# A two-block network on one core: other batch sizes for the gate projection inside the recurrent core

## The reference, cut to what matters

```python
h = rms_norm(x, norm_mix[l])
proj = h @ w_in[l]
u_pool, q, k, v, p_rw, gate_logits = jnp.split(proj, IN_SPLITS, axis=-1)
b_pool = pool_mixer(u_pool, pool_w[l], pool_scale[l])
b_da = diff_attention(q, k, v, lam, lambda_init, da_subln[l])
b_rw = rwkv7_mixer(p_rw, ...)                      # S = S*w + (S a) b + v k, token by token
branches = jnp.stack([b_pool, b_da, b_rw], axis=2)
up = jnp.einsum('blnc,ncd->blnd', branches, w_branch[l])
gates = jax.nn.sigmoid(gate_logits.reshape(B, L, 3, D_MODEL))
merged = jnp.sum(gates * up, axis=2)
x = x + merged @ w_out[l]
x = x + conv_glu_ffn(rms_norm(x, norm_ffn[l]), ...)
```

## Time and profile before

| | |
|---|---|
| median of 3 runs | 2748.31 us (2746.76 to 2751.6) |
| profiled execution: time and span | the span is 2750.0 us; the profile gives no time beside it |
| PE busy | 2680.6 us, 97% of the span |
| DVE / ACT / POOL busy | 1828.3 / 1134.2 / 354.4 us |

### The profile page before, as it was taken

One profiled execution on the slowest core, in us unless ns is written; L12 is line 12 of the kernel. 1 busy time (PEld: TensorE's weight loads), 2 busy tenths in 40 slices (PEclk: granted clock), 3 DMA queues, 4 the chain that ended last, 5 costly groups with the idle time before them and its releaser, 6 DMA issues.

```text
span 2750.0 us, 58101 instructions
## 1 busy us (share of the span) xinstructions
PE 2680.6 (97%) x25663; PEld 2454.4 (89%) x25663; DVE 1828.3 (66%) x2782; ACT 1134.2 (41%) x1844; POOL 354.4 (13%) x213
## 2 busy tenths in 40 slices
PE   8998999999999999999999999999999999999998
PEld 8987898999999999988899899999987788877886
DVE  7743345555888846844444455888845998888887
ACT  6332324534333323532424543433323346466664
POOL 1210122121111100210122121011100000010001
PEclk9999999999999999999999999999999999999999
DMA  4210222255333343211222154344332322499996
GB/s 148 81 43 23 82 77 76 71 189 183 116 128 133 127 137 124 80 54 36 59 87 82 57 173 145 100 138 134 134 101 94 93 92 69 161 359 391 390 393 257
DMA packets 113186, 372.28 MB, mean 135 GB/s; under 512 B 12560, under 2 KB 13728, under 8 KB 112544
## 3 DMA queue, kind: packets, MB, share of 16 engines
q1 hardware_dynamic: 88848, 304.04, 32.4%
q10 hardware_dynamic: 17568, 40.84, 4.2%
q0 software_dynamic: 6512, 23.62, 2.3%
HBM read 336.51 MB, written 31.94 MB: 134 GB/s over the span
## 4 chain that ended last, share of the span: by engine, by line
PE 83%; DVE 9%; ACT 4%; issue 2%; DMA 2%; POOL 0%; ACTq 0%; DVEq 0%; SPq 0%; POOLq 0%
PE PS L320 81%; DMA RING<-wts 1%; DVE RINGR L315 1%; DVE HR L486 1%; DVE ARENA L850 0%; ACT ARENA L412 0%; PE PS L3236 0%; PE PS L1394 0%; ACT HIGHR L304 0%; DVE ARENA L1737 0%; PE PS L920 0%; DVE ARENA L852 0%; DVE H L496 0%; DVE ARENA L1183 0%; DVE ARENA L817 0%
## 5 line engine op out<-in xcount | busy, mean ns | idle before, releaser
L320 PE MATMUL PS<-HR,HIGHR 128*128 128x264 f32 (+1 forms) x2976 | 846.0, 284 | 2.0 <-issue 2.0
L320 PEld LDWEIGHTS PS<-HR,HIGHR 128*128 128x128 f32 x2976 | 562.3, 189 | 5.4 <-issue 2.4
L320 PE MATMUL PS<-XR,HIGHR 128*128 128x264 f32 (+2 forms) x1760 | 552.9, 314 | 6.5 <-ACT STAGE L616 5.3
L320 PE MATMUL PS<-XR,RINGR 128*128 128x264 f32 (+1 forms) x1568 | 446.4, 285 | 0.0
L304 ACT CAST HIGHR<-RING 128x1024 fp32r<-128x1024 f32 (+2 forms) x340 | 330.5, 977 | 245.6 <-DMA RING<-wts 108.9
L320 PE MATMUL PS<-HH,HIGHR 128*128 128x264 f32 (+2 forms) x1472 | 424.5, 288 | 2.8 <-DVE RINGR L315 1.4
L320 PE MATMUL PS<-HH,RINGR 128*128 128x264 f32 (+2 forms) x1472 | 421.4, 286 | 0.0
L315 DVE TENSOR_TENSOR RINGR<-RING,HIGHR 128x1024 fp32r<-128x1024 f32 (+2 forms) x272 | 307.8, 1137 | 118.7 <-ACT HIGHR L304 118.4
L320 PEld LDWEIGHTS PS<-XR,HIGHR 128*128 128x128 f32 x1760 | 333.1, 189 | 31.0 <-issue 10.0
L320 PE MATMUL PS<-ARENA 64*64 64x64 f32 (+8 forms) x8666 | 303.0, 232 | 24.4 <-issue 22.0
L320 PEld LDWEIGHTS PS<-ARENA 64*64 64x64 f32 (+5 forms) x8666 | 256.8, 138 | 61.2 <-issue 28.0
(11 more groups left out here) (442 smaller groups left out, 5204.8 us busy)
## 6 DMA issues: line engine op xcount, KB each, us to landing
RING<-wts SPq DMA_DIRECT2D x324, 512.0 KB, 3.6
ARENA<-wmoe SPq DMA_DIRECT2D x204, 512.0 KB, 6.8
RING<-wts SPq DMA_DIRECT2D x52, 256.0 KB, 2.9
gates<-STAGE ACTq DMA_DIRECT2D x48, 264.0 KB, 4.2
ARENA<-gates ACTq DMA_DIRECT2D x48, 264.0 KB, 3.0
ys<-RING ACTq DMA_DIRECT2D x16, 512.0 KB, 7.0
RING<-wts SPq DMA_DIRECT2D x16, 384.0 KB, 3.0
ys<-STAGE POOLq DMA_DIRECT2D x8, 512.0 KB, 6.5
```

The source lines that it names most:

```text
L320: return e.matmul(out, lhsT, rhs, start=start, stop=stop, skip_group_check=True)
```

## The change

`beside` gets its number of steps at every place. The 11 places of a tile of 128 tokens had 1 step each; now they have 3 behind the turns and ML, 0 behind C, D and NT, 3 behind AT4, A4 and NV, 2 behind A8 to Y2, 3 behind Q, 3 behind E, ET and R, 3 behind X and EE, 3 behind XX, 0 behind GY, and 2 ahead of chunk 0's FS and 0 ahead of chunk 1's: 22 steps in eight batches. The tile of 16 tokens keeps 3 at each of its places. No line of another engine's program changes; their fill calls follow the steps.

```diff
-        beside = lambda n=1: fill(n if j else 3)
+        beside = lambda n: fill(n if j else 3)
...
         turn(2, k.Kf, banks.place(w, key("turn"), 2))
-        beside()
+        beside(3)
...
         banks.emptied_by(b, 2, "core_dve", key("NT"))
-        beside()
+        beside(0)
...
         banks.emptied_by(b, 2, "core_act", key("NV"))
-        beside()
+        beside(3)
...
         product("Y2", k.bDI, k.bC, 0, 0, "core_act", key("Y2"))
-        beside()
+        beside(2)
         w.wait_ge(*A[key("Y1")])
         w.wait_ge(*A[key("Y2")])
         product("Q", k.bD, k.bY, 0, away, "core_dve", key("Q"))
-        beside()
+        beside(3)
...
         wide("R", k.bQ, k.U0, away, 0)
-        beside()
+        beside(3)
...
             product("EE", k.bE, k.bET, 0, 1, "core_dve", key("EE"))
-            beside()
+            beside(3)
...
             wide("XX", k.bEEI, k.U2, 1, 0)
-            beside()
+            beside(3)
...
         if j:
-            beside()
+            beside(0)
...
         for c in ck:
-            beside()
+            beside(0 if c else 2)
```

## The result

Before 2747.5 us, changed 2774.7 us in the median of four runs each; ratio 1.009 (95% interval 1.0074 to 1.0106), so 27 us slower (25 by the ratio). The forecast was 2781. The profiled execution of the changed kernel has a span of 2773.0, against 2750.0: 23 us are to be found in the traces.

A forecast was written before the change was run, and what follows sets the result against it. PE, busy for 97% of the span, was taken to bound the kernel. Terms 57.6 + 4.8 - 6.5 - 5.8 + 5.6 - 26.8 + 3.8 = +32.7 us, added to the median 2748.31, gave 2781; range 2763 to 2801.

The forecast's parts named there:

- The core's steps: Core tiles: 0.72 us a further step, 2.40 a batch of three; +7.2 a tile, +57.6 in eight tiles.
- Rival (2): Core takes added steps for nothing, in hidden waits; tile growth under 2.2 us decides; 2741 us, chance 0.06.
- Relief: Core: longer batches let late copies and issue stalls catch up; a quarter of the idle 25.8 us, -6.5.
- The rule weighed in the prediction: Skill's rule: crossing into blocks of 256 instructions is mostly hidden; relief would be 0, the sum 6.5 us higher.
- Gaps left bare: Core: AT4 waits 0.35 to 0.4, none behind GY, 0.2 between chunks; 0.6 us a tile, +4.8.
- `finish()`: Four steps a layer taken from `finish()`, 0.72 us each with PE bound; -5.8 us for both layers.
- The attention: Unit 17: group 2's sums make DVE 5.0 us late, 2.2 spare; +2.8 a layer, +5.6.
- The tail: Behind the last unit: 40 fewer steps, but the merge begins only 13.4 us earlier instead of 28.8; -26.8 in both layers.
- one wait of some 15 us: Sign: at each layer's first merge product PE waits once on DVE, some 15 us, the largest in the kernel.
- The clock: An idle 15 us brings a fall to the lower clock once a layer; +3.8 us, bounds 0 and 8.
- (1): Rival: the merge's wait isn't there, as ACT is faster or PE has other work; 2746 us, no change, chance 0.09.
- (3): Rival: in the core POOL holds DVE up at line 1168; all 11 meetings cost +19, 2800 us, chance 0.13.

The follow-up runs named there:

- eleven in eight batches: Kernel before with its 11 steps a tile grouped in the change's eight places, three gaps bare, none added; 2736.4 us, ratio 0.9971.
- two steps everywhere: Changed kernel's 22 steps a tile as 2 at each of the eleven places, no gap bare; 2768.5 us, ratio 1.0085 against the kernel before.
- the run with halved units: Changed kernel with 1 + 1 instead of 2 + 2 steps in 19 attention units, 38 steps a layer back behind the last; 2748.5 us, ratio 1.0011.
- fourteen steps: Changed kernel with 14 instead of 22 steps a tile in eight batches, 45 left behind the last unit; 2737.4 us, ratio 0.9968 against before.
- sixteen steps: Changed kernel with 16 instead of 22 steps a tile in the same eight batches; 2731.3 us, ratio 0.9948; again on another chip 2733.7, 0.9957.

## Why the prediction was right, and where its sizes were off

Right in sign and in the main mechanism: PE got 88 steps in the cores at nearly full price, and the steps that left the tail bought back less than half, since the merge waits for ACT and DVE. The number was 6 us high by the medians, 10 by the two profiles. That it was so near is in part luck: the cores were put 15 us too high and the attention 10.5 too low, and the two nearly cancel.

**The core's steps.** 7.2 a tile by price of a batch; a batch of three measured 2.35. From eleven in eight batches to the changed kernel (busy 179.92 to 226.68 us in six tiles) a further step costs 0.71 of PE, for which the forecast had 0.72. Rival (2), steps for nothing, is refuted: the threshold was 2.2 a tile, the tiles grew by 4.9.

**Relief**, the mis-sized term. I took 6.5 us of 25.8. Idle time in six tiles fell by 9.5, 12.7 for eight. On top, PE's busy time grew by 38.7 in six tiles, not by 43.2 (6 x 7.2). Eleven steps in eight batches show why: the grouping saves 1.7 a tile, 1.3 of it in busy time, where the batch prices say 0.7. The rule weighed in the prediction, by which relief would be 0, doesn't hold here (last section).

**Gaps left bare.** Forecast 0.35 to 0.4 at AT4; measured 3.5 us in ten waits, 0.4 at most. No wait behind GY is in the list. That two steps everywhere gave the same time agrees.

**`finish()`.** The stage with the fourth tile and these steps grew by 7.0, forecast 8.2; all of the growth is in layer 1, so that this agreement shows little.

**The attention.** 5.6 forecast, 16.1 measured: the second error. The time of the sums was right to 0.1 us. What failed is the cover and the wait. I let PE's second batch of that unit be two steps of 0.72, and it holds a pooling output (0.7 us). I took the wait to be for DVE at the next transposes, with 2.2 us to spare; it is for ACT's exponential at the next unit's scores, where there was less to spare (the other 0.7). And I gave no clock's fall to a wait of 3 us; it came in both layers, 6.8 us each.

**The tail.** Forecast -26.8, measured -30.3 (-14.7 and -15.6). ACT's casts ran on beside the three transfers, 4.5 us for both sets where I had 6.0, and DVE's eight low parts set the merge. Of the idle time that I had called one wait of some 15 us, 9.7 stand there; 5.8 stand earlier, at the banks of outputs 2 and 3. ACT set those too, so the sum wasn't touched. What I had given as the sign of it, one wait of some 15 us on DVE, came only as one of 9.7.

**The clock.** Forecast 3.8, from one stall. The lower level lasted from 552.0 to 565.6 and from 1616.9 to 1634.0. PE idled most of that away; from the merge on it ran 4.2 us in each layer at half speed, which loses 4.2 in both. That is the forecast's size; the falls in the attention, some 5 in both layers, were in no term.

**Rivals (1) and (3).** The merge's wait is there, 9.7 us a layer, and the run with halved units shows its price: without it and its like, no change. For (3), DVE's line 1168 in the changed kernel, beside the earlier trace rows:

```profile
L1168 DVE TENSOR_TENSOR ARENA<-ARENA,CST x30: 268/682/2507, 121.0 to 1339.6; 128x512 f32<-128x512 f32 x24, 16x128 f32<-16x128 f32 x6
```

By line and form the 24 of 512 columns average 929 ns, before 727; POOL's busy time in six tiles went from 22.02 to 43.37. So the meetings came, nearly 5 us of them, and PE waited for none. The rival is refuted as a cost, not as a mechanism.

**What is open.** Whether fourteen steps, without any wait at the merge, are slower than sixteen isn't settled, nor why they don't gain by the missing wait. The profiles put it down to stalls in the cores, but no run moved those alone. The same holds for layer 1 paying more than layer 0. Nor did a run take the clock's falls away by themselves.

## What to carry to other kernels

When filler work is moved from a late stage into an early one, it costs its full price there (0.71 us a step here), and its gain is capped by how early the engine that ends the late stage can be ready: walk that engine's list, tables and all, before counting. Move until a long wait appears and stop: sixteen steps gain 14 us (8 of them by the grouping alone), twenty-two lose 27. And look at which wait ends last and what each cover consists of, for a batch of two steps isn't 1.4 us where the steps are another product's.

## What the runs showed of the hardware

**Stalls lie at edges of blocks of 256 instructions.** I counted all of PE's 51858 records in the order of time as one list: products, weight loads, and the 532 of its sequencer. Nearly every gap above 0.65 us that no engine explains comes at number 194 or 195 modulo 256 (115 of 117 in all 13 profiles, and all the 115 in the cores):

```
kernel   start of gap, us, number modulo 256
before   209.5 2.46 194;  231.8 1.92 194;  269.4 1.69 194;  284.7 2.04 195;  1238.3 2.47 195
changed  155.5 0.78 195;  256.2 1.59 194;  278.9 1.85 194;  1260.0 1.31 194;  1281.7 3.00 194
fourteen 190.2 2.20 195;  248.8 2.99 194;  1282.1 1.77 195
```

The page's table of queues (packets, MB, share) has the instructions' own transfers:

```profile
q8 instruction: 204, 3.34, 0.5%
```

204 packets of 16.4 KB for 51858 records are 254 records each. In the records PE goes on 2.2 to 3.3 us behind the start of such a transfer. Short products run through half a block, 64 products and 64 loads, in about 1.1 us; filler steps of 0.12 us a product take 7.7. So longer batches would let the fetch catch up, and where the edge falls in the tile would decide what a layer pays. That it is the fetch is argued from the places and the starts of transfers; no run here changed the fetch itself, and none shifted the edges alone. The Trainium skill ("Runtime: NRT & Kernel Launch", "Instruction fetch mechanics") gives the same blocks of 256 and calls the crossing "mostly hidden"; that agrees outside the cores, beside long products, where none of the 115 gaps stands, and not beside short ones, where they reach 3.0 us in the rows above.

**The granted clock falls with short waits.** With 4.2 us of waiting in the attention came 6.8 us at the lower level, with 15.5 us of waits in the tail 13.7 in layer 0 and 17.1 in layer 1.

**A change of tables costs its 1.28 us and no more.** In ACT's rows behind the last unit the load at 549.18 begins 0.02 us behind the end of the exponential ahead of it, and the tanh starts 0.02 us behind the load's end. The Trainium skill ("ScalarE: Activation LUTs", "What ACT_TABLE_LOAD costs") gives 1.28 us for the load, which agrees, and another 1.38 to drain the engine ahead of it, of which these rows show nothing. By the page's figure, as an estimate, the five changes of this stage would make ACT's chain some 7 us longer than it is.
